# Gate units of a fused block: norm products spread out, running sums moved to later units, decayed factors on VectorE, two stores awaited by their reader

## Chip, cores and metric
One NeuronCore of a Trainium2 chip runs the whole program. The metric is the device time of one execution in microseconds, as the median of several runs; lower is better.

## The reference
The function is three transformer blocks in a row on a sequence of 512 tokens of width 1024, all in float32. The change lies in the second block. It applies a SwiGLU layer, projects the normed result, and cuts the projection into a part for an RWKV-7 branch, a part for sliding window attention, and two gates:

```python
p_rwkv, p_att, p_gate = jnp.split(proj, [RWKV_COLS, RWKV_COLS + ATT_COLS], axis=-1)
y_rwkv = rwkv7_branch(p_rwkv, ...)
y_att = attention_branch(p_att, ...)
gate_rwkv, gate_att = jnp.split(jax.nn.sigmoid(p_gate), N_BRANCH, axis=-1)
merged = gate_rwkv * (y_rwkv @ w_branch_rwkv[l]) + gate_att * (y_att @ w_branch_attn[l])
```

Inside the RWKV branch, a key `kk = k * k_k` is divided by its norm per head of 64 channels, and a recurrence over time uses a decay per step. The kernel computes the recurrence in pieces of 64 tokens. For that it needs the running sum of the log decay inside each piece, the exponentials of that sum with both signs, and r, k, kk and a scaled by them (here called the decayed factors). The branch also adds a bonus, `sum(r * k * r_k) * v`. The attention branch needs q and k divided by their root mean square per head.

## The kernel before
The second block's projection is the class `Mix` (from line 3175), the last of four stages in one program region ("middle"). After it a region boundary (a barrier of all engines, line 84) leads to `branch_stage` (line 734), which holds recurrence and attention; another boundary leads to the region "later", which begins with `Join` (line 3438).

**Layout.** Channels lie on the 128 partitions and the 512 tokens on the free dimension, so a block is 128x512 numbers. `RWB` is 4 (blocks of the RWKV width), `NQ` is 5 (four blocks of q and one of k), `NL` is 12 (small products of the low-rank parts), `GB2` is 16 (gate blocks).

**Units.** All large products run in a common scheme, `Flow` (line 1180). One unit makes one output block from 8 blocks of input. Weights come from DRAM into a ring of 4 buffers (SyncE issues them). ScalarE rounds them to a high part (`split_high`, line 1291, one 128x1024 operation per unit), VectorE subtracts to get the low part (`split_low`, line 1299), and TensorE does 24 matmuls of 128x512 (line 1351: high times low, low times high, high times high). The high part has two buffers, so ScalarE splits the weights of unit u + 2 when TensorE has finished unit u.

**Gate units.** The last 16 units of `Mix`, numbered u = 0 to 15, make the gates. Every engine has its order of work written out by hand, unit by unit, and goes strictly through it:
- TensorE (`tensor`, line 3215): 24 matmuls, then in some units small products with a matrix that averages over a head (line 3232): two a unit in units 0 to 3 and one in unit 4 (four for the norm of kk, five for q and k), one in each of units 9 to 12 for the bonus. Small products go round three PSUM banks, so one waits until the third before it has been read.
- ScalarE (`scalar`, line 3285): `split_high` for u + 2; in units 0 to 4 square roots of the small products (lines 3325, 3329); in units 5 to 8 three exponentials of one block (lines 3334, 3335, 3337), which need VectorE's running sum of that block; then in `send` (line 3339) the sigmoid of the gate (line 3342) and the DMA that stores it (line 3344). Square root, exponential and sigmoid each need another activation table, so a unit with roots or exponentials has two table loads.
- VectorE (`vector`, line 3350, and `later`, line 3403): it takes the product out of PSUM with a multiplication (line 3399), does `split_low` for u + 2, and then `later(u)`: in units 0 to 3 a norm block (lines 3411 to 3413) and the running sum and a subtraction (lines 3415, 3416); in units 4 to 8 one block of q or k (lines 3422, 3423); in units 9 to 12 three multiplications (lines 3427, 3429, 3430); in units 11 to 14 the bonus (line 3435).
- GpSimd (`pool`, line 3262): bonus factors at the start, and after all exponentials eight multiplications that make decayed r and k (lines 3282, 3283).
- The front region, far earlier, ends with a store by ScalarE too (line 1820); there no engine waits for it before the boundary, its reader in the next region does (line 405).
- At the end (`finish`, line 3346) ScalarE waits until all 16 gate stores have landed; only then can the region end. `Join.load` (line 3465) reads the gates back in two DMAs after the recurrence.

The semaphore that ScalarE waits for before the exponentials of block b is `g_ready`, which VectorE raises after the subtraction of line 3416. The one that VectorE waits for before the multiplications of block b is `exps`.

Of the kernel before, what the change touches and what calls it, by code (L numbers as in the profile page):

```python
# [9 lines left out]
ALU = mybir.AluOpType  # L10
# [6 lines left out]
T = 512  # L17
# [102 lines left out]
def allocate_core(nc, ctx, ins):  # L120
# [2 lines left out]
    core.first_high = {"ssd": [nc.alloc_semaphore(f"ssd_first_high{n}") for n in range(2)], "middle": [nc.alloc_semaphore("middle_first_high")]}  # L123
    core.first_low = {"middle": [nc.alloc_semaphore("middle_first_low")]}
    core.last_c_out = nc.alloc_semaphore("last_c_out")
    core.first_weights = {name: [nc.alloc_semaphore(f"{name}_first_weights{n}") for n in range(count)] for name, count in (("ssd", 2), ("middle", 3))}
    sb = lambda name, shape: ctx.enter_context(nc.sbuf_tensor(name, shape, F32))
    core.ident = sb("ident", [P, P])
# [3046 lines left out]
class Mix:  # L3175


    NL, NQ = 3 * RWB, RWB + 1

    def __init__(self, rg, gates_dram):  # L3180
        self.rg, self.gates_dram, core, ins = rg, gates_dram, rg.core, rg.core.ins
# [40 lines left out]
    def tensor(self, pe):  # L3222
        rg, core, flow = self.rg, self.rg.core, self.flow
        NL, NQ = self.NL, self.NQ
        bonus, en = self.r7["bonus"], self.r7["en"]

        def product(n, w, x):
            if n >= 3:
                pe.wait_ge(self.small_free, n - 2)
            elif n == 0:  # L3230
                pe.wait_ge(self.into.rooted, 1)
            pe.matmul(self.small_bank(n)[:, :], w, x, start=True, stop=True).then_inc(self.small_done, 1)

        def after_att(u):
            if u == 0:
                pe.wait_ge(self.lora_in, 48)
                pe.wait_ge(self.lora_act, 2)
            for n in (2 * u, 2 * u + 1):
                q, b = divmod(n, RWB)
                up, x = self.loras[q]  # L3240
                product(n, up[:, b * P:(b + 1) * P], x)

        def after_gate(u):
            if u < 2:
                for b in (2 * u, 2 * u + 1):
                    pe.wait_ge(self.sq_ready, b + 1)
                    product(NL + b, core.mean_of_head[:], en[:, b, :])
            elif u < 5:
                for m in range(2 * u - 4, min(2 * u - 2, NQ)):
                    pe.wait_ge(self.qk_squared, m + 1)  # L3250
                    product(NL + RWB + m, core.mean_of_head[:], self.qk[m][1])
            elif 9 <= u < 9 + RWB:
                pe.wait_ge(self.bonus_in, u - 8)
                product(NL + RWB + NQ + u - 9, core.mean_of_head[:], bonus[:, u - 9, :])

        flow.multiply(pe, self.wa, lambda n: self.into.mean(pe, rg.banks[6], rg.acc))
        flow.multiply(pe, self.xg)
        flow.multiply(pe, self.rkv)
        flow.multiply(pe, self.attj, after_att)
        flow.multiply(pe, self.gate, after_gate)  # L3260

    def pool(self, pool):
        lora, shifted, reset = self.lora, self.shifted, self.reset
        r, kn, eg, en, bonus = shifted[:, 0:RWB, 1:T + 1], *(self.r7[n] for n in ("kn", "eg", "en", "bonus"))
        self.flow.wait_product(pool, self.down, DB - 1)
        pool.memset(reset, 1.0).then_inc(self.zeros, 1)  # L3266
        pool.memset(shifted[:, :, 0:1], 0.0).then_inc(self.zeros, 1)
        pool.memset(lora[:, :, 0:1], 0.0).then_inc(self.zeros, 1)
        pool.wait_ge(self.zeros, 3)
        pool.memset(reset.rearrange("p (c t) -> p c t", t=HEAD)[:, :, 0:1], 0.0).then_inc(self.zeros, 1)  # L3270
        build_masks(self.rg.core, Order(pool, self.p_order), self.masks, bonus)

        pool.wait_ge(self.v_done, 1)
        for b in range(RWB):
            pool.tensor_tensor(bonus[:, b, :], r[:, b, :], kn[:, b, :], ALU.mult).then_inc(self.pool_done, 1)
        for b in range(RWB):
            pool.wait_ge(self.pool_done, b + 1)
            pool.tensor_scalar(bonus[:, b, :], bonus[:, b, :], column(self.rg.core, "rwkv_r_k_2", b), None, ALU.mult).then_inc(self.bonus_in, 1)

        pool.wait_ge(self.exps, 3 * RWB)  # L3280
        for b in range(RWB):
            pool.tensor_tensor(r[:, b, :], r[:, b, :], eg[:, b, :], ALU.mult).then_inc(self.pool_done, 1)
            pool.tensor_tensor(kn[:, b, :], kn[:, b, :], en[:, b, :], ALU.mult).then_inc(self.pool_done, 1)

    def scalar(self, act):
        rg, core, flow, lora = self.rg, self.rg.core, self.flow, self.lora
# [29 lines left out]
        for u in range(gate.steps):  # L3316
            flow.split_high(act, gate.step0 + u + 2)
            if u == 0:
                flow.wait_emptied(act, attj, RWB + 1)
                for b, buf in self.qk:  # L3320
                    act.activation(buf, self.att[:, b, :], ACT.Square).then_inc(self.qk_squared, 1)
            if u < 2:
                for b in (2 * u, 2 * u + 1):
                    act.wait_ge(self.small_done, NL + b + 1)
                    act.activation(eg[:, b, :], self.small_bank(NL + b)[:, :], ACT.Sqrt, scale=float(HEAD)).then_inc(self.small_free, 1)
            elif u < 5:
                for m in range(2 * u - 4, min(2 * u - 2, NQ)):
                    act.wait_ge(self.small_done, NL + RWB + m + 1)
                    act.activation(self.qk[m][1], self.small_bank(NL + RWB + m)[:, :], ACT.Sqrt, bias=core.eps[:]).then_inc(self.small_free, 1)
            elif u < 9:  # L3330
                b = u - 5
                act.wait_ge(self.norm_done, RWB)
                act.wait_ge(self.g_ready, b + 1)
                act.activation(en[:, b, :], eg[:, b, :], ACT.Exp, scale=-1.0).then_inc(self.exps, 1)
                act.activation(lw[:, b, :], lw[:, b, :], ACT.Exp).then_inc(self.exps, 1)
                act.wait_ge(self.exps, 3 * b + 2)
                act.activation(eg[:, b, :], eg[:, b, :], ACT.Exp).then_inc(self.exps, 1)
            self.send(act, u)

    def send(self, act, n):  # L3340
        self.flow.wait_emptied(act, self.gate, n)
        act.activation(self.gate_out[n % 2], self.gate_out[n % 2], ACT.Sigmoid).then_inc(self.gate_made, 1)
        act.wait_ge(self.gate_made, n + 1)
        act.dma_start(self.gates_dram[:, n:n + 1, :], self.gate_out[n % 2]).then_inc(self.gate_sent[n % 2], 16)

    def finish(self, act):
        for sent in self.gate_sent:
            act.wait_ge(sent, 8 * GB2 + 16)

    def vector(self, dve):  # L3350
        rg, core, flow, lora, shifted = self.rg, self.rg.core, self.flow, self.lora, self.shifted
# [51 lines left out]
    def later(self, dve, order, u):  # L3403

        core, NL, NQ = self.rg.core, self.NL, self.NQ
        lw, eg, en, a, g, kk, kn, bonus = (self.r7[n] for n in ("lw", "eg", "en", "a", "g", "kk", "kn", "bonus"))
        v = self.shifted[:, 2 * RWB:3 * RWB, 1:T + 1]
        if u < 4:
            b = u
            dve.wait_ge(self.small_free, NL + b + 1)  # L3410
# [1 line left out]
            order.then(dve.reciprocal(en[:, b, :], eg[:, b, :]))  # L3412
            order.then(dve.tensor_tensor(kk[:, b, :], kk[:, b, :], en[:, b, :], ALU.mult))
            dve.sem_inc(self.norm_done, 1)
            order.then(dve.tensor_tensor_scan(eg[:, b, :], self.reset, lw[:, b, :], 0.0, ALU.mult, ALU.add))
            order.then(dve.tensor_tensor(lw[:, b, :], eg[:, b, :], lw[:, b, :], ALU.subtract))
            dve.sem_inc(self.g_ready, 1)
        elif u < 4 + NQ:
            m = u - 4
            b, buf = self.qk[m]  # L3420
            dve.wait_ge(self.small_free, NL + RWB + m + 1)
            order.then(dve.reciprocal(buf, buf))
            order.tick(dve.scalar_tensor_tensor(self.att[:, b, :], self.att[:, b, :], column(core, "attn_k_norm_2" if b == RWB else "attn_q_norm_2"),
                                                buf, ALU.mult, ALU.mult))
        elif u < 4 + NQ + RWB:
            b = u - 4 - NQ
            order.then(dve.tensor_tensor(a[:, b, :], a[:, b, :], kk[:, b, :], ALU.mult))
            dve.wait_ge(self.exps, 3 * b + 3)
            order.tick(dve.tensor_tensor(a[:, b, :], a[:, b, :], en[:, b, :], ALU.mult))
            order.tick(dve.scalar_tensor_tensor(kk[:, b, :], kk[:, b, :], -1.0, lw[:, b, :], ALU.mult, ALU.mult))  # L3430
        if 11 <= u < 11 + RWB:
            b = u - 11
            n = NL + RWB + NQ + b
            dve.wait_ge(self.small_done, n + 1)
            dve.scalar_tensor_tensor(bonus[:, b, :], self.small_bank(n)[:, :], float(HEAD), v[:, b, :], ALU.mult, ALU.mult).then_inc(self.small_free, 1)
# [2 lines left out]
class Join:  # L3438
# [25 lines left out]

    def load(self, sp):
        self.flow.load(sp, [self.attj], 0, RING)
        for half in (1, 0):
            sp.dma_start(self.gates[:, half * DB:(half + 1) * DB, :], self.gates_dram[:, half * DB:(half + 1) * DB, :]).then_inc(self.gates_in[half], 16)
        self.flow.load(sp, [self.attj], RING)
        self.flow.load(sp, self.jobs[1:])  # L3470
# [264 lines left out]
```

## Time and profile before

| | us |
|---|---|
| median of 3 runs | 3637.78 |
| lowest and highest | 3636.49, 3637.85 |
| the profiled execution | 3639.04 |
| its span, first to last instruction | 3637.3 |
| mean granted TensorE clock, as a share of full | 0.992 |

The profiled execution is 1.26 us above the median, and its span is 1.74 us shorter than its time. The span has 49271 instructions. The gate units lie between 1762 and 1875 us of it. In rows of the timeline the first number is the start, the second the duration; "[2.00 <-DVE arena L1299]" says that the engine was idle for 2.00 us and that the instruction of VectorE at line 1299 ended this.

### The profile page before, as it was taken

The page shows a single profiled execution, that of the slowest core. Times are in us where ns is not written, and L with a number is a line of the kernel's source. Part 1 is how long each engine was busy: PE and PEld are TensorE (multiplying, and loading weights), DVE is VectorE, ACT ScalarE, POOL GpSimd, SP SyncE. Part 2 cuts the span into 40 slices and gives each one's busy share as a digit, 9 for nine tenths or more (in the row PEclk, how much of TensorE's full clock was granted, in tenths as well). Part 3 has the DMA queues.
Part 4 walks back from the last instruction along what each step waited for, and adds up shares of the span by engine and source line. Part 5 has one row for each costly group of instructions (what it writes and reads, how often), then busy time and mean ns, then how long its engine had stood idle before and what let it go on. Part 6 is the DMA issues. An engine that isn't in the chain of part 4 may idle for free. (4 is left out here: it accounts for less than half of the span.)

```text
span 3637.3 us, 49271 instructions
## 1 busy us (share of the span) xinstructions
PE 3548.1 (98%) x20307; PEld 2918.0 (80%) x20307; DVE 2057.6 (57%) x2853; ACT 1509.3 (41%) x2407; POOL 357.4 (10%) x331
## 2 busy tenths in 40 slices
PE   8999999999999999999989899999999999999999
PEld 6888788888788888887668778888988887876887
DVE  6987687775534454446676563444364744366743
ACT  5564678543423332223543332223353323255322
POOL 3671000000000000002121000000000000153000
PEclk9999999999999999999999999999999999999999
DMA  6345644333233333333310233333223333411332
GB/s 206 94 134 171 199 130 141 114 93 98 82 98 99 93 94 98 95 96 98 87 59 3 80 96 99 98 93 105 87 82 97 95 98 88 140 47 47 98 94 86
DMA packets 597302, 364.79 MB, mean 100 GB/s; under 512 B 16823, under 2 KB 578823, under 8 KB 596567
## 3 DMA queue, kind: packets, MB, share of 16 engines
q1 hardware_dynamic: 592487, 349.91, 32.7%
q10 hardware_dynamic: 4592, 11.73, 0.8%
q8 instruction: 161, 2.64, 0.3%
q14 instruction: 62, 0.51, 0.0%
HBM read 345.70 MB, written 15.89 MB: 99 GB/s over the span
## 5 line engine op out<-in xcount | busy, mean ns | idle before, releaser
L1351 PE MATMUL later_bank<-arena 128*128 128x512 f32 (+1 forms) x6792 | 1435.6, 373 | 13.8 <-DVE arena L1299 10.6
L1351 PEld LDWEIGHTS later_bank<-arena 128*128 128x128 f32 x6792 | 1193.0, 188 | 250.2 <-DVE arena L1299 19.4
L1291 ACT ACTIVATE arena<-arena 128x1024 fp32r<-128x1024 f32 (+3 forms) x547 | 567.6, 1038 | 1536.7 <-PE later_bank L1351 756.9
L1351 PE MATMUL middle_bank<-arena 128*128 128x512 f32 x4896 | 1126.1, 391 | 5.8 <-DVE arena L1299 4.3
L1351 PEld LDWEIGHTS middle_bank<-arena 128*128 128x128 f32 x4896 | 916.5, 188 | 216.0 <-DVE arena L1299 12.6
L1299 DVE TENSOR_TENSOR arena<-arena 128x1024 fp32r<-128x1024 f32 (+3 forms) x549 | 666.2, 1213 | 558.7 <-ACT arena L1291 552.5
L1351 PE MATMUL front_bank<-arena 128*128 128x512 f32 (+3 forms) x1776 | 349.8, 356 | 7.6 <-DVE arena L1299 3.1
L1351 PEld LDWEIGHTS front_bank<-arena 128*128 128x128 f32 (+1 forms) x1776 | 291.2, 188 | 58.0 <-DVE arena L1910 3.9
L1544 POOL TENSOR_TENSOR arena<-arena 128x512 f32<-128x512 f32 x120 | 167.4, 1395 | 119.4 <-ACT arena L1847 103.4
L1351 PE MATMUL ssd_bank<-arena 128*128 128x512 f32 x576 | 144.0, 401 | 0.2 <-DVE arena L1299 0.2
L2004 DVE SCALAR_TENSOR_TENSOR arena<-front_bank,columns,arena 128x510 f32<-128x510 f32 (+1 forms) x224 | 126.7, 627 | 20.1 <-ACT arena L1774 19.1
L3266 POOL MEMSET arena<- 128x512 f32 x1 | 0.5, 527 | 1342.7 <-PE middle_bank L1351 1342.7
L1351 PEld LDWEIGHTS ssd_bank<-arena 128*128 128x128 f32 x576 | 107.0, 189 | 23.2 <-issue 1.4
L2033 DVE SCALAR_TENSOR_TENSOR front_bank<-arena,columns,front_bank 128x512 f32<-128x512 f32 x116 | 87.5, 754 | 3.9
L522 ACT ACTIVATE arena<-arena 128x128 f32<-128x128 f32 x240 | 76.0, 388 | 27.1 <-DMA arena<-scratch_cum 27.1
L1847 ACT ACTIVATE arena<-arena,columns 128x512 f32<-128x512 f32 x120 | 78.1, 717 | 2.1 <-ACT arena L1816 1.2
L2662 POOL TENSOR_SCALAR arena<-arena,small 128x128 f32<-128x128 f32 (+3 forms) x64 | 68.5, 1083 | 50.5 <-DVE small L2835 50.5
L2524 ACT ACTIVATE arena<-arena 128x512 f32<-128x512 f32 x32 | 20.2, 632 | 111.7 <-DVEq L2555 111.7
L2560 DVE TENSOR_TENSOR arena<-later_bank,arena 128x512 f32<-128x512 f32 x32 | 22.1, 692 | 78.1 <-PE later_bank L1351 78.1
L901 PEld LDWEIGHTS branch_bank<-arena 64*64 64x64 f32 x1792 | 55.4, 135 | 8.7 <-issue 7.3
L901 PE MATMUL branch_bank<-arena 64*64 64x64 f32 x1792 | 60.7, 220 | 0.0
L2118 DVE TENSOR_TENSOR arena<-arena 128x512 f32<-128x512 f32 x63 | 43.8, 695 | 21.0 <-ACT arena L2102 15.6
(484 smaller groups left out, 3040.7 us busy)
## 6 DMA issues: line engine op xcount, KB each, us to landing
arena<-in_w_in SPq DMA_DIRECT2D x114, 512.0 KB, 3.9
arena<-in_ffn_w_gate SPq DMA_DIRECT2D x76, 512.0 KB, 3.7
arena<-in_ffn_w_up SPq DMA_DIRECT2D x76, 512.0 KB, 3.7
arena<-in_w_mlp SPq DMA_DIRECT2D x64, 512.0 KB, 3.8
arena<-in_w_ada SPq DMA_DIRECT2D x48, 512.0 KB, 6.1
arena<-in_ffn_w_down SPq DMA_DIRECT2D x48, 512.0 KB, 3.9
arena<-scratch_cum SPq DMA_DIRECT2D x64, 256.0 KB, 6.5
arena<-in_gm_w_in SPq DMA_DIRECT2D x32, 512.0 KB, 3.9
```

Source lines behind the costliest of these rows:

```text
L522: ins = act.activation(seg[:, k, c, :], seg[:, k, c, :], ACT.Relu, scale=-1.0, bias=cum[:, c, h:h + 1])
L901: ins_ = pe.matmul(out[p, block_of(h)], left[p, h, :], right[p, h, :], start=True, stop=True)
L1291: act.activation(self.high[q % self.AHEAD][:, 0:kb * cols], self.raw[self.slot(g)][:, 0:kb * cols], ACT.Copy).then_inc(self.high_done, 1)
L1299: dve.tensor_tensor(self.low[self.slot(g)][:, 0:kb * cols], self.raw[self.slot(g)][:, 0:kb * cols], self.high[q % self.AHEAD][:, 0:kb * co ...
L1351: ins = pe.matmul(out, still, moving, start=first and n_pass == 0, stop=last and n_pass == 2)
L1544: order.then(pool.tensor_tensor(self.u[:, b, :], self.u[:, b, :], self.prod[:, m % self.PRODUCTS, :], ALU.add))
L1847: act.activation(self.prod[:, p % self.PRODUCTS, :].rearrange("p (s t) -> p s t", s=NSEG), tap, ACT.Copy, scale=column(core, "conv_dw_w", ...
L2004: ins = dve.scalar_tensor_tensor(dst, src, w, dst, ALU.mult, ALU.add)
L2033: self.mark = order.tick(dve.scalar_tensor_tensor(sums, tap, w, sums, ALU.mult, ALU.add))
L2118: dve.tensor_tensor(rg.acc, rg.acc, rg.squares[n % 2], ALU.add).then_inc(self.added, 1)
L2560: dve.tensor_tensor(self.whole[:, n, :], flow.bank(up, n), self.whole[:, n, :], ALU.mult).then_inc(flow.emptied["dve"], 1)
L2662: pool.tensor_scalar(buf, buf, self.rden[:, m % NJ:m % NJ + 1], None, ALU.mult).then_inc(self.normed, 1)
```

## The change
Four things change. The products for norms come one a unit (two in unit 0), in units 0 to 7, and ScalarE's roots with them. VectorE's running sums and subtractions move from units 0 to 3 into units 9 to 12, and with them ScalarE's exponentials from units 5 to 8 into 9 to 12; the multiplications that use them come one unit later (10 to 13), and the bonus products go to units 8, 11 and 12. The decayed r and k are made by VectorE in units 13 and 14 and no longer by GpSimd. ScalarE's end waits for the first 14 stores only; the last two have semaphores of their own, for which SyncE waits in `Join.load`.

```diff
@@ class Mix
+    BONUS_PRODUCTS = {8: (0, 1), 11: (2,), 12: (3,)}
+    BONUS_AT = {9: (0, 1), 13: (2,), 14: (3,)}
+    DECAYED_AT = {13: (0,), 14: (1, 2, 3)}
+    FIRST_SCAN = RWB + NQ
@@ tensor
         def after_gate(u):
-            if u < 2:
-                for b in (2 * u, 2 * u + 1):
-                    pe.wait_ge(self.sq_ready, b + 1)
-                    product(NL + b, core.mean_of_head[:], en[:, b, :])
-            elif u < 5:
-                for m in range(2 * u - 4, min(2 * u - 2, NQ)):
-                    pe.wait_ge(self.qk_squared, m + 1)
-                    product(NL + RWB + m, core.mean_of_head[:], self.qk[m][1])
-            elif 9 <= u < 9 + RWB:
-                pe.wait_ge(self.bonus_in, u - 8)
-                product(NL + RWB + NQ + u - 9, core.mean_of_head[:], bonus[:, u - 9, :])
+            for b in (0, 1) if u == 0 else range(u + 1, min(u + 2, RWB)):
+                pe.wait_ge(self.sq_ready, b + 1)
+                product(NL + b, core.mean_of_head[:], en[:, b, :])
+            m = u + 1 - RWB
+            if 0 <= m < NQ:
+                pe.wait_ge(self.qk_squared, m + 1)
+                product(NL + RWB + m, core.mean_of_head[:], self.qk[m][1])
+            for b in self.BONUS_PRODUCTS.get(u, ()):
+                pe.wait_ge(self.bonus_in, b + 1)
+                product(NL + RWB + NQ + b, core.mean_of_head[:], bonus[:, b, :])
@@ pool
-        pool.wait_ge(self.exps, 3 * RWB)
-        for b in range(RWB):
-            pool.tensor_tensor(r[:, b, :], r[:, b, :], eg[:, b, :], ALU.mult).then_inc(self.pool_done, 1)
-            pool.tensor_tensor(kn[:, b, :], kn[:, b, :], en[:, b, :], ALU.mult).then_inc(self.pool_done, 1)
@@ scalar (the roots move with the products)
...
-            elif u < 9:
-                b = u - 5
+            b = u - self.FIRST_SCAN
+            if 0 <= b < RWB:
                 act.wait_ge(self.norm_done, RWB)
                 act.wait_ge(self.g_ready, b + 1)
@@ send, finish
-        act.dma_start(self.gates_dram[:, n:n + 1, :], self.gate_out[n % 2]).then_inc(self.gate_sent[n % 2], 16)
+        sent = self.gate_sent if n < GB2 - 2 else self.rg.core.last_gates_out
+        act.dma_start(self.gates_dram[:, n:n + 1, :], self.gate_out[n % 2]).then_inc(sent[n % 2], 16)
...
-            act.wait_ge(sent, 8 * GB2 + 16)
+            act.wait_ge(sent, 8 * GB2)
@@ later
             order.then(dve.tensor_tensor(kk[:, b, :], kk[:, b, :], en[:, b, :], ALU.mult))
             dve.sem_inc(self.norm_done, 1)
-            order.then(dve.tensor_tensor_scan(eg[:, b, :], self.reset, lw[:, b, :], 0.0, ALU.mult, ALU.add))
-            order.then(dve.tensor_tensor(lw[:, b, :], eg[:, b, :], lw[:, b, :], ALU.subtract))
-            dve.sem_inc(self.g_ready, 1)
...
-        elif u < 4 + NQ + RWB:
-            b = u - 4 - NQ
+        b = u - self.FIRST_SCAN
+        if 0 <= b < RWB:
+            order.then(dve.tensor_tensor_scan(eg[:, b, :], self.reset, lw[:, b, :], 0.0, ALU.mult, ALU.add))
+            order.then(dve.tensor_tensor(lw[:, b, :], eg[:, b, :], lw[:, b, :], ALU.subtract))
+            dve.sem_inc(self.g_ready, 1)
             order.then(dve.tensor_tensor(a[:, b, :], a[:, b, :], kk[:, b, :], ALU.mult))
+        b = u - self.FIRST_SCAN - 1
+        if 0 <= b < RWB:
             dve.wait_ge(self.exps, 3 * b + 3)
             order.tick(dve.tensor_tensor(a[:, b, :], a[:, b, :], en[:, b, :], ALU.mult))
             order.tick(dve.scalar_tensor_tensor(kk[:, b, :], kk[:, b, :], -1.0, lw[:, b, :], ALU.mult, ALU.mult))
-        if 11 <= u < 11 + RWB:
-            b = u - 11
+        for b in self.DECAYED_AT.get(u, ()):
+            dve.wait_ge(self.bonus_in, RWB)
+            dve.wait_ge(self.exps, 3 * b + 3)
+            order.tick(dve.tensor_tensor(r[:, b, :], r[:, b, :], eg[:, b, :], ALU.mult))
+            order.tick(dve.tensor_tensor(kn[:, b, :], kn[:, b, :], en[:, b, :], ALU.mult))
+        for b in self.BONUS_AT.get(u, ()):
@@ Join.load
         self.flow.load(sp, [self.attj], 0, RING)
+        for sent in self.rg.core.last_gates_out:
+            sp.wait_ge(sent, 16)
```

## Rows read from the trace of the kernel before

**Rows 1.** The page, first part: busy time of each engine over the span.
```profile
PE 3548.1 (98%) x20307; PEld 2918.0 (80%) x20307; DVE 2057.6 (57%) x2853; ACT 1509.3 (41%) x2407; POOL 357.4 (10%) x331
```

**Rows 2.** Timeline of TensorE in the gate units.
```profile
1775.10 1.88 PE L3232 MATMUL middle_bank<-arena,mean_of_head 128*128 128x512 f32 x4
1776.42 6.02 PE L1351 MATMUL middle_bank<-arena 128*128 128x512 f32 x24
...
1799.87 7.41 PE L1351 MATMUL middle_bank<-arena 128*128 128x512 f32 x24 [2.00 <-DVE arena L1299]
1808.46 23.09 PE L1351 MATMUL middle_bank<-arena 128*128 128x512 f32 x96 [1.19 <-DVE arena L1299]
1831.39 1.02 PE L3232 MATMUL middle_bank<-arena,mean_of_head 128*128 128x512 f32 x2
1831.85 6.04 PE L1351 MATMUL middle_bank<-arena 128*128 128x512 f32 x24
1837.73 1.02 PE L3232 MATMUL middle_bank<-arena,mean_of_head 128*128 128x512 f32 x2
```

**Rows 3.** Windows: stretch, its length, busy PE, PEld, DVE, ACT, POOL, clock, DMA.
```profile
1802.00:1805.00 3.00, 3.00 (x10) 2.39 (x9) 2.82 (x3) 2.13 (x3) 0.00 (x0) 0.62 0.00 0
```

**Rows 4.** Timeline of VectorE in the gate units.
```profile
1778.72 1.23 DVE L3415 TENSOR_TENSOR_SCAN arena<-arena 128x512 f32<-128x512 f32 x1
1779.98 0.69 DVE L3416 TENSOR_TENSOR arena<-arena 128x512 f32<-128x512 f32 x1
1780.81 0.69 DVE L3399 TENSOR_TENSOR arena<-middle_bank,arena 128x512 f32<-128x512 f32 x1
1781.42 1.21 DVE L1299 TENSOR_TENSOR arena<-arena 128x1024 fp32r<-128x1024 f32 x1
1782.55 0.42 DVE L3411 TENSOR_SCALAR arena<-arena 128x512 f32<-128x512 f32 x1
...
1789.40 0.69 DVE L3399 TENSOR_TENSOR arena<-middle_bank,arena 128x512 f32<-128x512 f32 x1 [0.22 <-DVE arena L3416]
...
1806.59 0.69 DVE L3399 TENSOR_TENSOR arena<-middle_bank,arena 128x512 f32<-128x512 f32 x1 [0.22 <-DVE arena L3416]
...
1835.51 0.68 DVE L3399 TENSOR_TENSOR arena<-middle_bank,arena 128x512 f32<-128x512 f32 x1
...
1859.93 1.22 DVE L1299 TENSOR_TENSOR arena<-arena 128x1024 fp32r<-128x1024 f32 x1 [0.39 <-ACT arena L1291]
...
1869.72 0.69 DVE L3399 TENSOR_TENSOR arena<-middle_bank,arena 128x512 f32<-128x512 f32 x1 [4.15 <-PE middle_bank L1351]
```

**Rows 5.** Timeline of ScalarE in the gate units.
```profile
1786.28 1.28 ACT L3342 ACT_TABLE_LOAD   x1
1790.12 0.63 ACT L3342 ACTIVATE arena<-arena 128x512 f32<-128x512 f32 x1 [2.56 <-DVE arena L3399]
...
1809.47 1.28 ACT L3334 ACT_TABLE_LOAD   x1
1810.77 0.63 ACT L3334 ACTIVATE arena<-arena 128x512 f32<-128x512 f32 x1
...
1814.98 1.06 ACT L1291 ACTIVATE arena<-arena 128x1024 fp32r<-128x1024 f32 x1 [0.46 <-ACT arena L3342]
...
1837.99 1.06 ACT L1291 ACTIVATE arena<-arena 128x1024 fp32r<-128x1024 f32 x1 [1.13 <-PE middle_bank L1351]
...
1858.84 1.06 ACT L1291 ACTIVATE arena<-arena 128x1024 fp32r<-128x1024 f32 x1 [5.55 <-PE middle_bank L1351]
...
1871.11 0.33 ACTq L3344 DMA_DIRECT2D scratch_gates<-arena  x1
```

**Rows 6.** Timeline around two region boundaries: front to ssd, then middle to branch.
```profile
421.27 0.33 ACTq L1820 DMA_DIRECT2D scratch_b_and_c<-arena  x1
...
423.19 0.82 SPq L397 DMA_DIRECT2D arena<-scratch_cum  x2
...
1874.78 0.35 SPq L798 DMA_DIRECT2D small<-in_attn_sinks  x1
```

More of the change, by code:

```diff
@@ L125, in allocate_core @@
     core.last_c_out = nc.alloc_semaphore("last_c_out")
+    core.last_gates_out = [nc.alloc_semaphore(f"last_gates_out{n}") for n in range(2)]
     core.first_weights = {name: [nc.alloc_semaphore(f"{name}_first_weights{n}") for n in range(count)] for name, count in (("ssd", 2), ("middle", 3))}
@@ L3263, in pool @@
         lora, shifted, reset = self.lora, self.shifted, self.reset
-        r, kn, eg, en, bonus = shifted[:, 0:RWB, 1:T + 1], *(self.r7[n] for n in ("kn", "eg", "en", "bonus"))
+        r, kn, bonus = shifted[:, 0:RWB, 1:T + 1], self.r7["kn"], self.r7["bonus"]
         self.flow.wait_product(pool, self.down, DB - 1)
@@ L3321, in scalar @@
                     act.activation(buf, self.att[:, b, :], ACT.Square).then_inc(self.qk_squared, 1)
[L3322 to L3329, printed above, removed]
-            elif u < 9:
-                b = u - 5
+            for b in (0, 1) if u == 0 else range(u + 1, min(u + 2, RWB)):
+                act.wait_ge(self.small_done, NL + b + 1)
+                act.activation(eg[:, b, :], self.small_bank(NL + b)[:, :], ACT.Sqrt, scale=float(HEAD)).then_inc(self.small_free, 1)
+            m = u + 1 - RWB
+            if 0 <= m < NQ:
+                act.wait_ge(self.small_done, NL + RWB + m + 1)
+                act.activation(self.qk[m][1], self.small_bank(NL + RWB + m)[:, :], ACT.Sqrt, bias=core.eps[:]).then_inc(self.small_free, 1)
+            b = u - self.FIRST_SCAN
+            if 0 <= b < RWB:
                 act.wait_ge(self.norm_done, RWB)
@@ L3406, in later @@
         lw, eg, en, a, g, kk, kn, bonus = (self.r7[n] for n in ("lw", "eg", "en", "a", "g", "kk", "kn", "bonus"))
-        v = self.shifted[:, 2 * RWB:3 * RWB, 1:T + 1]
+        r, v = (self.shifted[:, n * RWB:(n + 1) * RWB, 1:T + 1] for n in (0, 2))
         if u < 4:
```

## The prediction
> **What bounds the kernel now.** I read the page first: TensorE is busy for 98% of the span [rows 1], so only idle or slow stretches of it, and barriers, are to be had. The timeline of the gate units shows where these are. TensorE waits 2.00 us for VectorE's low weights before unit 5 and 1.19 us before unit 6 [rows 2]. The unit between them took 7.41 us where four units in a row took 22.93 (1808.46 to 1831.39), 5.73 each [rows 2], and the granted clock of a stretch inside it was 0.62 [rows 3], so most of it ran at 1.2 GHz: about 1.7 us more. VectorE is late because each of units 1 to 3 takes it 8.59 us (1780.81 to 1789.40), while units 4 to 8 take 28.92 us for five, 5.78 each (1806.59 to 1835.51) [rows 4]. Lastly, the final store is issued at 1871.11 [rows 5] and the next region starts at 1874.78 [rows 6], 3.67 us later. What the change can take is thus some 5 to 7 us inside the units and a part of these 3.67.
>
> **Units 0 to 8.** VectorE loses scan and subtraction. In unit 0 they took it from 1778.72 to 1780.81, 2.09 us [rows 4], so units 1 to 3 become 8.59 - 2.09 = 6.50. Unit 1 then starts at 1778.72, unit 4 at 1798.22, and with 5.78 each unit 9 at 1827.12. TensorE: a unit with one small product takes 6.34 (1831.39 to 1837.73), two products together 1.32 (1775.10 to 1776.42), and a unit right behind a product 5.88 (1831.85 to 1837.73) [rows 2]. From the product behind unit 1, at 1775.10 as before, seven such periods lead to 1819.48, the two bonus products to 1820.80, and unit 9 ends at 1826.68. VectorE's lows stay ahead: low 5 is made in VectorE's unit 3, which starts at 1778.72 + 2 x 6.50 = 1791.72, and is done 1.8 us later (0.61 for the take, 1.22 for the split), at 1793.5; TensorE wants it at 1775.10 + 3 x 6.34 + 0.46 = 1794.6. So both waits and the slow unit go. Before, unit 9 ended at 1831.39 [rows 2]: 4.7 us are won here. The new roots' table loads (two in each of units 0 to 7 now) cost nothing: ScalarE's unit is then about 5.4 us, under TensorE's 6.34.
>
> **Units 9 to 12: a loop closes.** In unit u VectorE's scan stands behind its split of weights u + 2, which needs ScalarE's high part. ScalarE's exponentials of the same unit now wait for that scan, and ScalarE's next split stands behind exponentials, sigmoid and store. Before, the sums were made units ahead and this loop was open. Its length:
> - ScalarE's split to VectorE's split: 1.09 (1858.84 [rows 5] to 1859.93 [rows 4]).
> - VectorE's split to its next operation: 1.13 (1781.42 to 1782.55); scan to subtraction 1.26 (1778.72 to 1779.98); subtraction to the next instruction 0.83 (to 1780.81) [rows 4]. I add 0.05 for the signal; my estimate.
> - ScalarE from the first exponential to the next split: 1810.77 to 1814.98, 4.21 [rows 5]. It has three exponentials, one table load, sigmoid and store.
>
> The sum is 8.57 us a unit against TensorE's 5.73. I leave out the first table load (1.28): in unit 2 it ran at 1786.28, and the operation behind it waited 2.56 us for VectorE until 1790.12 [rows 5], so a load runs ahead of the wait and hides under the scan. The loop begins with ScalarE's split in unit 9, 0.26 behind TensorE (1837.73 [rows 2] to 1837.99 [rows 5]), at 1826.94. VectorE, free of its take at 1827.73, is in time for it at 1828.03. Four rounds of 8.57 bring ScalarE's last split, that of weights 15, to 1861.22.
>
> **The tail.** VectorE's last split starts at 1862.31. TensorE's unit 15 starts 1.27 later at 1863.58 and ends at 1869.31, even if units 13 and 14 stood for some 1.5 and 3 us. But VectorE has more to do: in unit 13 behind the split (1.13) five multiplications, in unit 14 the take and seven more, each 0.61 start to start (1780.81 to 1781.42 [rows 4]): 1.13 + 5 x 0.61 + 8 x 0.61 = 9.06. So the last take is at 1871.37, not at 1869.72 [rows 4]: TensorE no longer ends this stretch, VectorE does. The last store is issued 1.39 behind the take (1869.72 [rows 4] to 1871.11 [rows 5]), at 1872.76: 1.65 us later than before. The 4.7 us won are all given back in the loop, and more.
>
> TensorE's pauses may bring the clock down to 1.2 GHz again, as the 2.00 us one did. In units 13 and 14 this costs nothing, since the loop and not TensorE sets the pace, and in unit 15 the 1.7 us would bring TensorE's end to 1871.0, still under 1871.37. So the clock has no term here.
>
> **GpSimd's eight multiplications** leave an engine that the boundary did not wait for; VectorE's eight are the ones counted above.
>
> **The store wait.** The nearest row is the end of the front region, where ScalarE's last act is also a store that only its reader awaits: issue at 421.27, next region at 423.19 [rows 6], 1.92 us. In place of 3.67 this saves 1.75. The bounds are 0 (the barrier still waits for the queue) and 3.67. SyncE's new waits in `Join.load` come after the whole recurrence, over 150 us behind these stores: nothing.
>
> **Sum.** +1.65 - 1.75 = -0.1 us, against the profiled execution of 3639.04. That one lies 1.26 above the median, and I carry the difference over: 3637.78 - 0.1, so **3637.7 us**. What a measurement of this kernel can tell from no change is 0.2%, 7.3 us.
>
> **Rivals.**
> - *The table load runs behind the wait* (semaphore first, then load). Then each round is 1.28 longer, 5.1 in all: 3642.8. Against it speaks the row at 1786.28; for it, that two waits stand before this exponential and one before that sigmoid.
> - *Slower: a change of table costs ScalarE double.* The place is the two changes in each round of the loop, the price another 1.30 each (1809.47 to 1810.77 [rows 5]), 8 x 1.30 = 10.4 us: 3648.1. It decides from 0.9 us a change on, where 8 x 0.9 passes 7.3. Against it: the exponential starts 1.30 behind the start of its load, with no room for more. The Trainium skill has such a rule, "ScalarE: Activation LUTs", section "What ACT_TABLE_LOAD costs": 1283 ns and about 1380 ns of drain for every switch. By it the time would be 11.0 us above mine; the trace shows the first part (1.28) and not the second.
> - *The loop does not bind.* If ScalarE's split got ahead in some way, TensorE would run through: 1826.68 + 6 x 5.73 + 2 x 0.61 = 1862.28, last take 0.2 later, 7.2 us before 1869.72, and with the store -9.0: 3628.8. This is the gain that the moved work would have without the loop. Against it speaks the order of `scalar` and `vector`, which leaves no way round.
> - *The store wait does not go*, because the end of a region waits for its queues: 3639.4. Against it, the front region's 1.92.
>
> **How the numbers follow.** My forecast 0.73, the late table load 0.11, double tables 0.03, open loop 0.04, store wait kept 0.09. My forecast's own spread: 0.2 us a round on the loop's handovers (0.8), 0.5 on when it begins, 1 on the boundary, in which the branch's first products also find another clock; so some 2.5 either way. The range takes in the late load and the kept wait: 3635.0 to 3643.5. Faster by over 0.2% is the open loop, 0.04. Slower by over 0.2% is the double table or the late load with the kept wait and some of the spread, 0.05. Within it, 0.91.
>
> **What would show it.** In the profile after: TensorE never waits in units 1 to 8 and unit 9 ends near 1826.7; ScalarE's splits in units 9 to 13 stand 8.6 us apart, with its first exponential waiting about 2 us for VectorE's subtraction behind an early table load; TensorE waits before units 13, 14 and 15; the last take is by a VectorE that was busy, near 1871.4; the boundary is near 1.9 us. I am wrong if splits in units 9 to 13 stand 6 us apart (open loop) or 9.9 (late load), or if the branch region starts more than 1.5 us away from 1874.7.

## The result and the profile after

The changed kernel takes 3643.79 us (median of 20 runs, 3639.74 to 3648.20) against 3638.14 for the kernel before (20 runs, 3636.06 to 3644.64). The ratio is 1.0014, with a 95% interval of 1.0008 to 1.0020: slower by 0.14%, some 5 us (5.65 between the medians), clear of the noise but under the 0.2% that the prediction took as its bound. The forecast was 3637.7 in a range of 3635.0 to 3643.5, so the time lies just outside it. The rival with the late table load had 3642.8.

The page after answers [rows 1]:

```profile
span 3641.8 us, 49282 instructions
PE 3550.1 (97%) x20307; PEld 2920.3 (80%) x20307; DVE 2059.1 (57%) x2861; ACT 1518.0 (42%) x2413; POOL 345.1 (9%) x323
```

ScalarE has gained six table loads and VectorE eight multiplications, which GpSimd has lost. Since the executions differ by several us in parts that the change doesn't touch, I measure the stretch itself in the traces: from the start of gate unit 0 to the first instruction of the branch region. It took 112.72 us before (1762.06 to 1874.78) and 117.39 after (1761.14 to 1878.53): 4.67 more, which is the loss.

TensorE after, for [rows 2]; unit 8 starts at 1812.68, units 9 to 11 stand in one row:

```profile
1812.68 6.04 PE L1352 MATMUL middle_bank<-arena 128*128 128x512 f32 x24
1818.56 1.88 PE L3237 MATMUL middle_bank<-arena,mean_of_head 128*128 128x512 f32 x4
1819.88 16.90 PE L1352 MATMUL middle_bank<-arena 128*128 128x512 f32 x72
1836.62 1.02 PE L3237 MATMUL middle_bank<-arena,mean_of_head 128*128 128x512 f32 x2
1838.19 5.76 PE L1352 MATMUL middle_bank<-arena 128*128 128x512 f32 x24 [0.55 <-DVE arena L1300]
1843.78 1.02 PE L3237 MATMUL middle_bank<-arena,mean_of_head 128*128 128x512 f32 x2
1848.02 5.72 PE L1352 MATMUL middle_bank<-arena 128*128 128x512 f32 x24 [3.21 <-DVE arena L1300]
1857.84 8.31 PE L1352 MATMUL middle_bank<-arena 128*128 128x512 f32 x24 [4.11 <-DVE arena L1300]
1867.66 5.75 PE L1352 MATMUL middle_bank<-arena 128*128 128x512 f32 x24 [1.51 <-DVE arena L1300]
```

No wait stands in units 1 to 9. ScalarE's split for unit 9 starts at 1825.99, so unit 9 ended 0.26 earlier, 64.6 us after unit 0 began; before it was 69.33 (1762.06 to 1831.39). The gain of 4.7 us is there. Then units 12 to 15 start 9.8 us apart, each waiting for VectorE's low weights.

ScalarE after, units 9 and 10, for [rows 5]:

```profile
1825.99 1.06 ACT L1292 ACTIVATE arena<-arena 128x1024 fp32r<-128x1024 f32 x1 [4.23 <-PE middle_bank L1352]
1830.31 1.28 ACT L3332 ACT_TABLE_LOAD   x1 [3.25 <-DVEq L3425]
1831.60 0.63 ACT L3332 ACTIVATE arena<-arena 128x512 f32<-128x512 f32 x1
...
1835.82 1.06 ACT L1292 ACTIVATE arena<-arena 128x1024 fp32r<-128x1024 f32 x1 [0.46 <-ACT arena L3340]
1840.13 1.28 ACT L3332 ACT_TABLE_LOAD   x1 [3.25 <-DVEq L3425]
```

This is the line that the forecast had otherwise. ScalarE is done with its split at 1827.05 and then idles 3.25 us for VectorE's signal (line 3425 raises `g_ready`); only then does it load the table, 1.28 us, and only then come the exponentials. The pitch of its splits is 9.83 us.

VectorE after, for [rows 4]: the start of unit 9 and the tail.

```profile
1826.19 0.68 DVE L3398 TENSOR_TENSOR arena<-middle_bank,arena 128x512 f32<-128x512 f32 x1
1827.08 1.23 DVE L1300 TENSOR_TENSOR arena<-arena 128x1024 fp32r<-128x1024 f32 x1 [0.21 <-ACT arena L1292]
1828.22 1.22 DVE L3423 TENSOR_TENSOR_SCAN arena<-arena 128x512 f32<-128x512 f32 x1
1829.48 0.69 DVE L3424 TENSOR_TENSOR arena<-arena 128x512 f32<-128x512 f32 x1
...
1836.91 1.23 DVE L1300 TENSOR_TENSOR arena<-arena 128x1024 fp32r<-128x1024 f32 x1 [3.98 <-ACT arena L1292]
...
1866.38 1.23 DVE L1300 TENSOR_TENSOR arena<-arena 128x1024 fp32r<-128x1024 f32 x1 [3.97 <-ACT arena L1292]
...
1875.34 0.68 DVE L3398 TENSOR_TENSOR arena<-middle_bank,arena 128x512 f32<-128x512 f32 x1
```

Both halves of the loop are to be seen: ScalarE waits 3.25 us for VectorE's sum in each of the four rounds, and VectorE 3.97 or 3.98 for ScalarE's split from the second on (0.21 in the first). The last take has no idle time before it, so VectorE's tail and not TensorE ends the units.

The clock, for [rows 3]: a row of the windows view, whose last three numbers are granted clock, DMA share and GB/s.

```profile
1858.00:1861.00 3.00, 3.00 (x8) 2.32 (x9) 2.79 (x4) 1.22 (x1) 0.00 (x0) 0.50 0.00 0
```

The boundary, for [rows 6], from the timeline of ScalarE's and SyncE's queues:

```profile
1876.71 0.33 ACTq L3343 DMA_DIRECT2D scratch_gates<-arena  x1
...
1878.53 0.35 SPq L799 DMA_DIRECT2D small<-in_attn_sinks  x1
```

TensorE's pause of 4.11 us before unit 14 was followed by 1.2 GHz; the unit took 8.31 us and cost nothing, since the next weights came only at 1867.66. The boundary fell from 3.67 to 1.82 us.

### The profile page after: what moved, and what is told of

Read it like the earlier page. It is cut to its first block and busy times, and to the rows that moved or that the text cites. A ratio compares the mean times of both kernels' runs of the same rounds, so it can differ in the third digit from the quotient of the medians.

```text
span 3641.8 us, 49282 instructions
## 1 busy us (share of the span) xinstructions
PE 3550.1 (97%) x20307; PEld 2920.3 (80%) x20307; DVE 2059.1 (57%) x2861; ACT 1518.0 (42%) x2413; POOL 345.1 (9%) x323
```

## The experiments

The question was why the pitch (the time from one ScalarE split to the next) is 9.83, and whether that pitch, VectorE's tail or the boundary makes the loss. Beside each time I give the stretch from unit 0 to the branch region ("stretch"): 112.72 before, 117.39 after.

**1. One wait.** The wait for the norms is implied by the later wait for the sum.

```diff
             if 0 <= b < RWB:
-                act.wait_ge(self.norm_done, RWB)
                 act.wait_ge(self.g_ready, b + 1)
```

> The changed kernel without ScalarE's wait for the norms in front of the exponentials (the wait for the running sum, which comes later on VectorE, implies it), so one wait is left there. Nothing computed changes. Theory A (the loop of units 9 to 12 sets the pace, and its first table load stands behind the wait because two waits stand there): the load runs ahead and hides under the scan, ScalarE's splits in units 9 to 13 go from 9.83 us apart to 8.55, and the time falls by 4 x 1.28 = 5.1 us against the changed kernel, to about 3638.5, the time of the kernel before within 1.5. Theory B (the load stands behind any wait for VectorE's sum, however many waits there are): splits stay 9.83 apart and the time stays near 3643.7. Theory C (the loss is the tail of multiplications on VectorE, not the loop): no change either, near 3643.7.

Measured: 3637.28 us, ratio 0.9996 (0.9987 to 1.0005). Stretch 112.03. ScalarE's timeline in unit 9:

```profile
1824.44 1.06 ACT L1292 ACTIVATE arena<-arena 128x1024 fp32r<-128x1024 f32 x1 [4.24 <-PE middle_bank L1352]
1825.52 1.28 ACT L3331 ACT_TABLE_LOAD   x1
1828.71 0.63 ACT L3331 ACTIVATE arena<-arena 128x512 f32<-128x512 f32 x1 [1.91 <-DVEq L3424]
...
1832.93 1.06 ACT L1292 ACTIVATE arena<-arena 128x1024 fp32r<-128x1024 f32 x1 [0.46 <-ACT arena L3339]
```

The load now runs at once, under VectorE's scan, and the exponential waits 1.91 us behind it. The pitch is 8.49, and the stretch is 5.36 shorter (4 x 1.34). Theories B and C are out: the place of one table load in each of four rounds is worth more than the whole loss of 4.67.

**2 and 3. The waits swapped**, in a single run and then in eleven.

```diff
-                act.wait_ge(self.norm_done, RWB)
                 act.wait_ge(self.g_ready, b + 1)
+                act.wait_ge(self.norm_done, RWB)
```

> The changed kernel with its two waits in front of the exponentials in the other order: the running sum first, the norms last. Theory A in the form that it is the number of waits: the load stays behind both, splits stay 9.83 us apart. If it is the last wait that rides on the operation and all else stands alone: the running sum now stands alone, and the load is behind it too, also 9.83. If only the first of several waits stays in front of the load: the pitch stays as well. A pitch of 8.55 would say that the order of the waits counts and not their number.

> The changed kernel with its two waits in front of the exponentials swapped, timed. In its first trace the splits stood 8.49 us apart, with the table load ahead of the wait for the running sum. Theory A, in the form that only the first of two waits stays behind the load: 5.3 us under the changed kernel, near 3638.3, like the kernel with one wait. Rival: the one time of 3634.3 was right and the swap gains more than the loop's 5.3: below 3636.

Measured: 3634.34 (one run) and 3638.71 (median of 11), ratio 0.9998 (0.9989 to 1.0007); stretches 112.03 and 112.06. In the timed one's trace, ScalarE in unit 9:

```profile
1825.60 1.06 ACT L1292 ACTIVATE arena<-arena 128x1024 fp32r<-128x1024 f32 x1 [4.23 <-PE middle_bank L1352]
1826.68 1.28 ACT L3332 ACT_TABLE_LOAD   x1
1829.87 0.63 ACT L3332 ACTIVATE arena<-arena 128x512 f32<-128x512 f32 x1 [1.91 <-DVEq L3425]
```

All forms of theory A that I had written for the single run said 9.83 and were wrong: it is not the number of waits. The order decides. Written last of two, the wait for the sum holds the load back; written first, or alone, it holds only the exponential. The same work in another order is worth 5.3 us in the stretch.

**4. The changed kernel again**, beside these.

> The changed kernel as it is, once more, beside the next run on the same chip. All theories: 3643.8 as before, splits 9.83 us apart.

Measured: 3643.57 us, ratio 1.0013 (1.0004 to 1.0022), stretch 117.37. In this trace TensorE waited 4.10 us before unit 15 and the unit took 7.32 us, to 1876.20. VectorE's last take came at 1876.56, so the slow unit was covered and the stretch is the same.

**5. The sums a unit earlier** on VectorE, so that ScalarE finds them made.

```diff
-        b = u - self.FIRST_SCAN
+        b = u - self.FIRST_SCAN + 1
         if 0 <= b < RWB:
             order.then(dve.tensor_tensor_scan(eg[:, b, :], self.reset, lw[:, b, :], 0.0, ALU.mult, ALU.add))
             order.then(dve.tensor_tensor(lw[:, b, :], eg[:, b, :], lw[:, b, :], ALU.subtract))
             dve.sem_inc(self.g_ready, 1)
+        b = u - self.FIRST_SCAN
+        if 0 <= b < RWB:
             order.then(dve.tensor_tensor(a[:, b, :], a[:, b, :], kk[:, b, :], ALU.mult))
```

> The changed kernel with scan and subtraction of each block one unit earlier on VectorE (units 8 to 11), the exponentials where they are (9 to 12). The loop is open: ScalarE finds the sum ready. Theory A: ScalarE's splits in units 9 to 13 stand 6.6 us apart (its own work in such a unit), TensorE hardly waits, the last take comes about 5 us earlier than in the kernel before, and with the store 1.85 us: about 3631.3, that is 12 us under the changed kernel and 7 under the kernel before. Theory C (tail): the tail of 4.9 us in unit 14 stays, and the time stays within 2 us of 3643.7.

Measured: 3631.86 us, ratio 0.9982 (0.9973 to 0.9991), stretch 105.65, 11.7 under the changed kernel. In the first round ScalarE still waited 1.20 us for the sum, with the load behind the wait (pitch 7.77). From then on it did not wait, and its splits stand 6.6 us apart:

```profile
1826.47 1.28 ACT L3332 ACT_TABLE_LOAD   x1 [1.20 <-DVEq L3425]
...
1831.98 1.06 ACT L1292 ACTIVATE arena<-arena 128x1024 fp32r<-128x1024 f32 x1 [0.46 <-ACT arena L3340]
...
1838.57 1.06 ACT L1292 ACTIVATE arena<-arena 128x1024 fp32r<-128x1024 f32 x1 [0.46 <-ACT arena L3340]
```

So the loop is the reason that the 4.7 us of units 0 to 8 did not reach the end.

**6. The store part alone**, in the kernel before (the edits of `send`, `finish` and `Join.load` in the diff above).

> The kernel before with only the store part of the change: ScalarE's end waits for 14 stores, SyncE in the later region for the last two. All theories: the boundary shrinks from 3.67 us to 1.82 as in the changed kernel, so 1.85 us faster than the kernel before, about 3636.3. If the branch region then starts at a lower TensorE clock or its loads collide with the stores, less than 1 us of it is left.

Measured: 3637.67 us, ratio 1.0000 (0.9991 to 1.0009). The interval is 6.5 us wide and cannot tell 1.85. The trace, which is of the fastest of the eleven runs (3630.80), can: stretch 110.86, 1.86 less than before, boundary 1.81.

**7. The store part undone**, in the changed kernel.

```diff
             act.wait_ge(sent, 8 * GB2)
+        for sent in self.rg.core.last_gates_out:
+            act.wait_ge(sent, 16)
```

> The changed kernel with its store part undone: ScalarE's end waits for all 16 stores again. All theories: the boundary grows from 1.82 us (last store issued to first instruction of the branch region) back to about 3.67, the units stay as they are, so about 1.85 us slower than the changed kernel, near 3645.6. If the end of a region waited for its queues anyway, the time would stay at 3643.8.

Measured: 3644.48 us, ratio 1.0017 (1.0008 to 1.0026), stretch 119.04 (1.65 more), boundary 3.48. In size as expected; in the medians 0.7 against the first measurement, not resolved.

**8. Decayed r and k on GpSimd again**, in the changed kernel (`DECAYED_AT = {}`, and the eight lines of `pool` of the kernel before).

> The changed kernel with the decayed r and k made by GpSimd again, after the last exponential (about 1862.9 in the changed kernel's trace). Theory A: the loop stays (splits 9.83 us apart); VectorE's tail is shorter by 8 x 0.6, so the last take follows TensorE's end at 1873.6 in place of 1875.3, 1.7 us sooner. GpSimd needs 8 x 1.3 to 1.9 us, till 1873.4 to 1878, so it may end the region itself: between 1.7 us faster and 1 us slower than the changed kernel, near 3642.5. Theory C (the moved multiplications are the cost of the change): it comes back to 3638 or below.

Measured: 3643.73 us, ratio 1.0008 (0.9999 to 1.0017), stretch 117.20, only 0.2 less. VectorE's tail was gone, but TensorE's last unit ran at the low clock:

```profile
1867.64 7.33 PE L1352 MATMUL middle_bank<-arena 128*128 128x512 f32 x24 [2.52 <-DVE arena L1300]
```

It took 7.33 us where the changed kernel's last unit took 5.75 in its first trace, and that 1.6 is what the shorter tail should have given. The trace thus speaks against theory C once more. It is of a run of 3644.74, though: three of the eleven runs took 3637.9 to 3638.9, no trace shows one of them, and what made them shorter is open.

**9. The tail spread**, on top of experiment 5, with one wait.

```diff
-    DECAYED_AT = {13: (0,), 14: (1, 2, 3)}
+    DECAYED_AT = {11: (0,), 12: (1,), 13: (2,), 14: (3,)}
...
-                act.wait_ge(self.norm_done, RWB)
```

> The kernel with the sums one unit earlier, and in addition one wait (not two) before the exponentials, and the decayed r and k made in units 11 to 14, one block each, in place of one in unit 13 and three in unit 14. Theory: in the kernel with the sums earlier the last take stood at 1861.8 behind VectorE's tail, while TensorE ended at 1859.9; with the spread tail the last take follows TensorE at 1860.1 or earlier, since the first exponential comes 1.2 us sooner too. So 1.7 to 2.5 us faster than that kernel, about 3629.7. Rival: VectorE's unit 11 (7 us of work) delays the weights and TensorE waits as much elsewhere: 3632.

Measured: 3630.01 us, ratio 0.9976 (0.9966 to 0.9986), stretch 102.67, 2.98 less than experiment 5 and 10.05 less than before. Of the 2.98, some 1.15 is that TensorE ends its units earlier (99.37 us after unit 0 began, against 100.52), and 1.84 is VectorE's tail, which had put the last take 1.94 behind TensorE's end and now puts it 0.10 behind. The two edits are not told apart. TensorE has no wait left in the units: its last three stand in one row.

```profile
1843.40 17.09 PE L1352 MATMUL middle_bank<-arena 128*128 128x512 f32 x72
1863.83 1.09 PE L832 MATMUL branch_bank<-ident,arena 128*128 128x128 f32 x4 [3.35 <-PEq L84]
```

**10. Norm products two a unit again**, on top of experiment 9: `after_gate` and ScalarE's roots with the conditions of the kernel before.

> The kernel with the spread tail with the norm products and ScalarE's roots two a unit again (units 0 to 4), all else kept. Theory A: the product part of the change is worth little, since the gain of units 0 to 8 comes from the sums taken out of VectorE's units 0 to 3. Units 0 to 3 take TensorE 7.17 us in place of 6.34 and units 5 to 7 5.73 in place of 6.34, so unit 9 ends within 1 us of where it did: 3630.0 to 3631.0. Rival: VectorE, which is behind in units 4 to 8, now holds TensorE up by 2 us before units 5 and 6 and the clock falls again: 3632 or more.

Measured: 3626.17 us (5 runs), ratio 0.9965 (0.9952 to 0.9977), stretch 102.49. The interval overlaps that of experiment 9; in the stretch the product part of the change is worth -0.2 us, nothing. The 3.8 us between the two medians is not this: the two traces differ by 1.35 us in the branch region and by 2.9 in the later one, where the clock was not the same (last section), and no edit was made there. The rival, a wait before units 5 and 6, did not come. This is the lowest median of the study, 0.35% under the kernel before, but part of that may be this clock, and it rests on five runs; it keeps the change's store part, the sums one unit before their reader and the decayed factors spread.

**11 and 12. Products behind the last unit** that nothing reads, six and two, on top of experiment 9, to keep TensorE busy up to the boundary.

```diff
         flow.multiply(pe, self.gate, after_gate)
+        pe.wait_ge(self.small_free, NL + RWB + NQ + 2)
+        for n in range(6):
+            pe.matmul(self.small_bank(NL + RWB + NQ + 1)[:, :], core.mean_of_head[:], self.reset, start=True, stop=True)
```

> The kernel with the spread tail, and six products of 128x512 behind TensorE's last unit that nothing reads (about 4 us, under VectorE's, ScalarE's and the boundary's own time). Nothing else is computed differently. Theory D: the first 2 to 10 us of the branch region run at 1.2 GHz because TensorE idled for 5.2 us at the boundary; the trace of the kernel before with the store part alone had 3.35 us of idle there, a granted clock of 1.00 and a branch region of 178.97 us against 181.4. So here the region takes 179.0 too, 2.4 us less: near 3627.3. Rival: the six products delay the boundary or the clock falls all the same: 3629.7 or up to 2 us more.

> The kernel with the spread tail and two products behind the last unit (not six) that nothing reads. In the trace with six they took 5.32 us and put the branch region 3.1 us later; two take about 1.8 us, which fits under the last take, sigmoid and store (1.5) and the boundary (1.8). Theory D: the idle time of TensorE at the boundary falls from 3.35 to about 2 us, the branch region starts at 2.4 GHz, its first 5.9 us become 4.5: about 1.4 us faster than with the spread tail alone, 3628.6. Rival: the clock still falls in most executions, or falls later in the region: 3630 as before.

Measured with six: 3632.11 us, ratio 0.9982 (0.9973 to 0.9991), a miss. They took 5.32 us and the stretch grew by 3.1; the branch region began at the full clock, yet took 182.73 us, since the clock fell to 0.69 in its last 19 us (2028.93 to 2047.93). With two (`range(2)`): 3630.00 us, ratio 0.9973 (0.9963 to 0.9983), stretch 102.67. The first products of the region then ran at 2.4 GHz and the region took 179.00 us against 180.33:

```profile
1864.01 0.63 PE L832 MATMUL branch_bank<-ident,arena 128*128 128x128 f32 x4 [1.63 <-PEq L84]
```

The medians of experiments 9 and 12 are the same, so the 1.3 us is seen in one trace and not shown in the time.

## Why the prediction was wrong

**The step that failed** is the sentence "I leave out the first table load (1.28) [...] so a load runs ahead of the wait and hides under the scan". It was read off the sigmoid, which has one wait before it, and carried over to the exponential, which has two. The prediction named this difference under its first rival and gave it 0.11. Experiments 1 to 3 show that the wait for the sum, as the last of two, stood before the load. The term was put at nothing and measured 1.34 us in each of four rounds (9.83 less 8.49), 5.36 in the stretch; the rival's forecast, with 4 x 1.28 = 5.1, was 3642.8.

**The loop itself** was right: the place, the units and the engines. With the load hidden its pitch was 8.49 against 8.57 forecast; with the load behind the wait 9.83 against the 9.9 that the text gave for the late load.

**Units 0 to 8**: 4.7 us forecast, 4.7 measured.

**The tail**: from VectorE's last split to the last take 9.06 forecast, 8.96 measured (1866.38 to 1875.34), and it was VectorE that ended the units. The prediction also said that this tail would cover a slow unit 15. So it was in experiment 4 (7.32 us, stretch unchanged), and without the tail (experiment 8) the low clock comes to the surface.

**The clock**: the pauses before units 13 and 14 were forecast as 1.5 and 3 us and were 3.2 and 4.1; with the pitch of 8.49 (experiment 3) they were 1.4 and 2.8. Unit 14 ran partly at 1.2 GHz and cost nothing, as said.

**The store wait**: 1.75 forecast, 1.85 measured.

**The open loop**, a rival, was put 9.0 us under the kernel before. Experiment 9, where ScalarE no longer waits, is 10.05 under it in the stretch. Most of the difference is the unit's time, read as 5.73 us from the four units behind a wait: three units without a wait take 16.74 us (1819.88 to 1836.62), 5.58 each, which over six units is 0.9 less by estimate. The forecast itself did not hang on this, as TensorE did not set the end.

**The doubled table price** did not come. The Trainium skill, "ScalarE: Activation LUTs", section "What ACT_TABLE_LOAD costs", gives 1283 ns and a drain of about 1380 ns. The trace agrees with the first and shows nothing of the second: from the start of the load to the start of its operation it is 1.29 us (1830.31 to 1831.60).

**The range** ended at 3643.5 and the median was 3643.79. It had held the late load (3642.8) and left 0.7 above it. Counted from the 3638.14 that 20 runs gave the kernel before, the 4.67 lost in the stretch gives 3642.8 as well. The last 1.0 lies outside the stretch, where no edit acts; what it is in the medians is not shown, but single traces differ there by up to 2.9 us (last section). The failed step alone put the time near the upper end; that it fell just outside and not just inside is chance.

## What to carry to other kernels

When work is moved to a later step, draw the circle of the waits it then stands in: here ScalarE's split, VectorE's split, VectorE's sum and ScalarE's exponentials each waited for the one before, 8.5 to 9.8 us a round where TensorE needed 5.7. Make the input one step ahead of its reader, as experiment 5 does, and the gain stays. Before an operation that needs another table, write the wait that ends last first; in experiments 2 and 3 the table load then ran under it.

## What was new about the hardware and the program

- Two waits in the other order moved a table load from behind the wait to ahead of it, 1.3 us a time. I did not look into what places it; the traces show only the three cases.
- After 3.35 us of idle at the boundary the branch region's first four products took 0.63 us (experiments 6 and 10) or 1.04 to 1.09 (8 and 9); after 3.6 they took 0.91 (experiment 1) or 1.09 (4); after 5.2 always 1.08 or 1.09, after 1.3 and 1.6 (11 and 12) 0.63. Where they took 0.63 the region took 178.97 to 179.00 us (182.73 in experiment 11), else 180.3 to 181.4.
- The later region, which none of these kernels changes but for two waits, took 1581.0 to 1582.2 us in nine of the traces and 1584.0 to 1584.1 in five (experiments 4, 5, 8, 9 and 12). All five show a granted clock of 0.96, and the nine 1.00, in two stretches of 40 us: 40 to 80 and 1160 to 1200 us behind the region's start. A share of 0.04 lost over 40 us is 1.6 us, so the two make some 3.2, my estimate, against 2.9 measured. Why the clock fell there in some executions is open. It is one reason for the several us between executions of one kernel: the two traces of the changed kernel lie on either side (1581.85 and 1584.02). The stretch comes out the same within 0.03 us where it was taken twice.
